# The attention mixer's output product, from float32 matmuls to three products of rounded parts and rests

## The reference, cut to what matters

```python
def attend(qb, k, v):
    s = jnp.einsum('bqhgd,bkhd->bhgqk', qb, k, preferred_element_type=F32) * scale
    p = jax.nn.softmax(s, axis=-1).astype(v.dtype)
    return jnp.einsum('bhgqk,bkhd->bqhgd', p, v)
...
o = lax.map(lambda qb: attend(qb, k_all, v_all), q_blocks)
y_lat = jnp.moveaxis(o, 0, 1).reshape(Bn, L, ATT_HEADS * dh) @ w_out    # 256x1024 times 1024x1024
```

## Time and profile before

| | |
|---|---|
| median of three runs | 2270.58 us |
| the profiled execution | 2269.32 us, of them 2267.5 us span |
| PE busy | 2183.9 us, 96% of the span |
| DVE, ACT busy | 1365.3 us (60%), 957.5 us (42%) |
| DMA | 373.10 MB, 165 GB/s on average |
| granted PE clock over the span | 0.987 |
| attention units, first scores to last mix | 811.2 to 852.5 us |
| output product | 853.3 to 881.2 us |
| feed-forward part begins | 895.3 us |

### The profile page before, as it was taken

One profiled execution on the slowest core, in us unless ns is written; L12 is line 12 of the kernel. 1 busy time (PEld: TensorE's weight loads), 2 busy tenths in 40 slices (PEclk: granted clock), 3 DMA queues, 4 the chain that ended last, 5 costly groups with the idle time before them and its releaser, 6 DMA issues. The chain is left out here.

```text
span 2267.5 us, 32554 instructions
## 1 busy us (share of the span) xinstructions
PE 2183.9 (96%) x13686; PEld 1868.4 (82%) x13686; DVE 1365.3 (60%) x1577; ACT 957.5 (42%) x1078; POOL 124.6 (5%) x69
## 2 busy tenths in 40 slices
PE   6999999999999998999999999999999999989999
PEld 4887788888888767888888898888988897878888
DVE  4357835756856364656665674566656686636665
ACT  3312424445544243444444463444444465234443
POOL 0066500000000000000000000000000011000000
PEclk8999999999999999999999999999999998999999
DMA  8327904554555302555555334554555442124552
GB/s 329 112 93 315 420 28 154 186 185 168 194 191 189 134 25 75 198 190 186 186 185 185 140 130 149 187 185 165 186 185 185 148 168 93 40 84 151 189 191 80
DMA packets 52529, 373.10 MB, mean 165 GB/s; under 512 B 5776, under 2 KB 6800, under 8 KB 7888
## 3 DMA queue, kind: packets, MB, share of 16 engines
q1 hardware_dynamic: 51632, 367.78, 44.7%
q0 software_dynamic: 800, 3.93, 0.5%
HBM read 370.64 MB, written 1.05 MB: 164 GB/s over the span
## 5 line engine op out<-in xcount | busy, mean ns | idle before, releaser
L375 PE MATMUL PS<-AR_r 128*128 128x512 f32 x2240 | 793.1, 398 | 1.5 <-DVE ring_r L502 1.5
L502 DVE TENSOR_TENSOR ring_r<-ring,AR_r 128x2048 fp32r<-128x2048 f32 x270 | 619.2, 2299 | 286.4 <-ACT AR_r L496 286.3
L496 ACT ACTIVATE AR_r<-ring 128x2048 fp32r<-128x2048 f32 x274 | 522.2, 1911 | 311.4 <-PE PS L394 193.6
L376 PE MATMUL PS<-AR_r,ring_r 128*128 128x256 f32 x2240 | 628.2, 280 | 0.0
L375 PEld LDWEIGHTS PS<-AR_r 128*128 128x128 f32 x2240 | 420.8, 188 | 105.4 <-DVE ring_r L502 2.3
L376 PEld LDWEIGHTS PS<-AR_r,ring_r 128*128 128x128 f32 x2240 | 422.8, 189 | 2.4
L554 ACT ACTIVATE AR<-PS 128x512 f32<-128x512 f32 x140 | 83.7, 598 | 439.7 <-PE PS L376 439.7
L392 PE MATMUL PS<-AR_r 128*128 128x512 f32 x616 | 242.3, 393 | 0.0
L394 PE MATMUL PS<-AR_r 128*128 128x512 f32 x616 | 240.9, 391 | 0.0
L393 PE MATMUL PS<-ring_r,AR_r 128*128 128x512 f32 x616 | 240.1, 390 | 0.0
L394 PEld LDWEIGHTS PS<-AR_r 128*128 128x128 f32 x616 | 115.6, 188 | 26.3
(11 more groups left out here) (390 smaller groups left out, 3027.9 us busy)
## 6 DMA issues: line engine op xcount, KB each, us to landing
ring<-stream SPq DMA_DIRECT2D x346, 1024.0 KB, 4.8
X<-xt SPq DMA_DIRECT2D x1, 2048.0 KB, 9.3
AR<-bias POOLq DMA_DIRECT2D x1, 1536.0 KB, 6.6
AR<-pt POOLq DMA_DIRECT2D x2, 512.0 KB, 3.6
out<-X SPq DMA_DIRECT2D x4, 256.0 KB, 2.1
SM<-small SPq DMA_DIRECT2D x1, 545.0 KB, 4.3
AR<-invc SPq DMA_DIRECT2D x1, 512.0 KB, 14.8
X<-negl POOLq DMA_DIRECT2D x1, 512.0 KB, 6.2
```

The source lines that it names most:

```text
L375: pe.matmul(PS[:, bank, :], w_hi, X_PARTS[:, :, k * T:(k + 1) * T], start=(k == 0), stop=False, skip_group_check=True)
L376: ins = pe.matmul(PS[:, bank, 0:T], w_lo, X_HI[:, k, :], start=False, stop=(k == DT - 1), skip_group_check=True)
L496: act.activation(w_hi_of(tag, i), ring[:, n % SLOTS, :], ACT.Identity).then_inc(split_hi, 1)
L502: dve.tensor_tensor(RING_R[:, n % SLOTS, :], ring[:, n % SLOTS, :], w_hi_of(tag, i), ALU.subtract).then_inc(split_lo, 1)
```

## The change

The output product is made from three fp32r products. Its four chunks are laid out anew: chunk 2h + part holds the features 4 part to 4 part + 3 (tiles of 128) by 512 output columns of half h, so that the matmuls are 128 x 512. The mixed heads are rounded by ACT into CAT1_HI (`round_heads`), and DVE writes the rest into CAT1_LO (`take_heads`). All four chunks are split, each with its own place for the rounded part. Chunks 0 and 1 are split in halves between the attention units, chunks 2 and 3 behind them. The two banks of the mixed pairs are exchanged, and PE's order in the product is half of the columns, half of the features, token tile.

```diff
-            if name.startswith(("ffn", "ple")) or name in ("mix0_in", "mix2_in", "mix3_in"):
+            if name.startswith(("ffn", "ple")) or name in ("mix0_in", "mix1_out", "mix2_in", "mix3_in"):
...
+        OUT1_HI = [arena(at, CHUNK_COLS, of=AR_R) for at in (16384, 18432, 20480, 22528)]
...
+        def act_split_half_chunk(act, order, tag, i, half):
+
+            n, cs = START[tag] + i, slice(half * 1024, (half + 1) * 1024)
+            need_chunk(act, n)
+            ins = act.activation(w_hi_of(tag, i)[:, cs], ring[:, n % SLOTS, cs], ACT.Identity)
+            if half:
+                act.wait_ge(order.sem, order.n)
+                ins.then_inc(split_hi, 1)
+            else:
+                ins.then_inc(order.sem, order.step())
...
-        CAT1 = arena(11264, AH, T)
+        CAT1_LO = arena(11264, AH, T, of=AR_R)
+        CAT1_HI = H_R[:, :, LAT]
+        MIX_BANKS = (0, 7)
...
-            pe.wait_ge(S["heads_taken"], S.at("heads_taken", 3))
-            for t in range(2):
-                for h in range(2):
-                    pe_tokens(pe, "mix1_out", "mix1_post", CAT1, 0, t, h, 2 * t + h, t == 1)
+            for h in range(2):
+                for part in range(2):
+                    i = 2 * h + part
+                    pe.wait_ge(split_lo, SPLIT_BASE["mix1_out"] + i + 1)
+                    w_hi, w_lo = OUT1_HI[i], RING_R[:, (START["mix1_out"] + i) % SLOTS, :]
+                    pe.wait_ge(S["heads_taken"], S.at("heads_taken", 2 if i == 0 else 3))
+                    for t in range(2):
+                        ts, o = slice(t * P, (t + 1) * P), PS[:, 2 * t + h, :]
+                        for k in range(4 * part, 4 * part + 4):
+                            w = slice(k % 4 * 512, (k % 4 + 1) * 512)
+                            pe.matmul(o, CAT1_HI[:, k, ts], w_hi[:, w], start=(k == 0), stop=False)
+                            pe.matmul(o, CAT1_HI[:, k, ts], w_lo[:, w], start=False, stop=False)
+                            ins = pe.matmul(o, CAT1_LO[:, k, ts], w_hi[:, w], start=False, stop=(k == DT - 1))
+                        if part and t == 0:
+                            ins.then_inc(S["tokens_done"], S.mark("tokens_done", ("mix1_post", t, h)))
+                    ins.then_inc(multiplied, 1)
...
+                if i in (4, 5, 8, 9):
+                    act_split_half_chunk(act, order, "mix1_out", i // 8, i % 2)
+                if i % 4 == 2 and i > 2:
+                    round_heads(act, i // 4 - 1)
+            round_heads(act, 3)
+            for i in (2, 3):
+                act_split_chunk(act, "mix1_out", i, free=START["mix1_in"])
+
+        def round_heads(act, hp):
+            act.wait_ge(S["head_mixed"], S.at("head_mixed", 2 * hp + 1))
+            act.activation(CAT1_HI[:, 2 * hp:2 * hp + 2, :], PS[:, MIX_BANKS[hp % 2], :].rearrange("p (a b) -> p a b", a=2),
+                           ACT.Identity).then_inc(S["heads_rounded"], S.mark("heads_rounded", hp))
...
+                if i in (5, 6, 9, 10):
+                    dve_split_half_chunk(dve, order, "mix1_out", (i - 5) // 4, (i - 5) % 2)
                 if i % 4 == 2 and i > 2:
                     take_heads(dve, i // 4 - 1)
             take_heads(dve, 3)
+            for i in (2, 3):
+                dve_split_chunk(dve, "mix1_out", i)

         def take_heads(dve, hp):
-            dve.wait_ge(S["head_mixed"], S.at("head_mixed", 2 * hp + 1))
-            dve.tensor_copy(CAT1[:, 2 * hp:2 * hp + 2, :].rearrange("p a b -> p (a b)"), PS[:, (7, 0)[hp % 2], :]).then_inc(S["heads_taken"], S.mark("heads_taken", hp))
+            dve.wait_ge(S["heads_rounded"], S.at("heads_rounded", hp))
+            heads = slice(2 * hp, 2 * hp + 2)
+            dve.tensor_tensor(CAT1_LO[:, heads, :], PS[:, MIX_BANKS[hp % 2], :].rearrange("p (a b) -> p a b", a=2), CAT1_HI[:, heads, :],
+                              ALU.subtract).then_inc(S["heads_taken"], S.mark("heads_taken", hp))
...
+def chunks_out_halves(w):
+
+    return w.reshape(2, 4, P, 2, 512).transpose(3, 0, 2, 1, 4).reshape(4, P, -1)
...
-    parts["mix1_out"] = chunks_in(g["att_w_out"][0])
+    parts["mix1_out"] = chunks_out_halves(g["att_w_out"][0])
```

More of the change, by code:

```diff
@@ L174, in build @@
         TURN_OF = {"ple2b": 2, "ple3b": 2, "ffn4": 1, "mix3_in": 1, "ffn1_lat": 2, "ffn2": 2, "mix2_in": 2}
-        w_hi_of = lambda tag, i: W0_HI[i % 3] if tag == "mix0_in" else W_HI[(i + TURN_OF.get(tag, 0)) % 3]
+        OUT1_HI = [arena(at, CHUNK_COLS, of=AR_R) for at in (16384, 18432, 20480, 22528)]
+        w_hi_of = lambda tag, i: OUT1_HI[i] if tag == "mix1_out" else W0_HI[i % 3] if tag == "mix0_in" else W_HI[(i + TURN_OF.get(tag, 0)) % 3]
         X_HI, X_LO = (arena(at, DT, T, of=AR_R) for at in (12288, 16384))
@@ L1214, in mix @@
                 for st in range(NCH):
-                    ins = pe.matmul(PS[:, (7, 0)[hp % 2], (h % 2) * T:(h % 2 + 1) * T], VV[:, st, (h // 4) * P:(h // 4 + 1) * P],
+                    ins = pe.matmul(PS[:, MIX_BANKS[hp % 2], (h % 2) * T:(h % 2 + 1) * T], VV[:, st, (h // 4) * P:(h // 4 + 1) * P],
                                     PT[:, h % 2, st, :], start=(st == 0), stop=(st == NCH - 1))
```

## The result

The kernel after takes 2275.51 us in the median of 7 runs (2272.05 to 2278.48), against 2270.58 before; the two medians lie 4.9 apart. The ratio on record is 1.0030, with a 95% interval of 1.0021 to 1.0039: 6.8 us slower, with 4.8 and 8.9 as the ends. Its profiled execution took 2277.11 us with a span of 2275.3; that of before 2269.32 and 2267.5.

The account below looks back on a forecast made before the run. PE alone bounds the output product, a PE-DVE loop the units. Units +8.4, product and earlier start -6.7, two clock falls +5.0: +6.7 us, 2277 us; own range 2274.5 to 2280, over the cases 8 in 10 between 2270 and 2281.

Parts of the forecast that it names:

- the falls: Clock drops to half speed after the long waits at units 5 and 9: two, 2.5 us each, 5.0 together; chance 0.60.
- The bound: Attention units: a loop through PE, DVE's maxima and scaling, 4.80 us for two units; work put between those lengthens it fully.
- The product: Output product: 96 matmuls at 0.230 us, as in the feed-forward row of the same form, take 5.7 us less.
- the start: Output product begins 1.04 us earlier, at 852.26 instead of 853.30, since its first quarter needs only the third pair of heads.
- The units: Attention units: added splits and pairs' rests delay PE by 3.19 + 0.52 + 3.16 + 0.52 + 1.0 = 8.4 us.
- The sum without falls: Delay in the units less the product's gain, clock drops left out: 8.4 - 6.7 = +1.7 us.
- The 3.6 us of idle time: PE idle at unit 5 from the end of unit 8's scores to 830.97; held long enough to bring a clock drop.
- the other five: Idle stretches of 2.8 to 4.7 us in PE's work in the trace; clock drops followed three of the five.
- half speed from 830.97 for 6.8 us: Price of a clock drop from unit 6's transposes on: 2.5 us each, bounds 1.5 and 3.4.
- 13.4: Sign in the timeline: the last mix that many us later than 850.53 with the clock drops, 8.4 without.
- the tail from 881.24 on stays as it is: Behind the product's last sums: remaining rounding, rests and chunks are done before them, so nothing was added there.
- the idle-time one: Rival: DVE's halves fit its 1.96 us waits before the maxima; only unit 14 costs 1.0, 5.7 us faster, 2264.9; chance 0.05.

Follow-up runs that it names:

- e4: The changed kernel with ACT's list alone altered: its halves of the first two chunks come after units 2, 4, 5 and 8; 2269.83 us, ratio 1.0005.
- e3: The changed kernel reordered: only the first chunk split between units, DVE's halves and two pairs' rests ahead of the maxima; 2267.36 us, ratio 0.9989.
- e1: The changed kernel with three filler score matmuls on PE in each long wait, before the transposes of units 6 and 10; 2273.48 us, ratio 1.0018.
- e8: The order of e3 with two filler score matmuls on PE between the last mix and the product; 2267.24 us, ratio 0.9996.
- e7: The kernel before, run again unaltered for a second timeline; one run, 2272.77 us.
- e9: The kernel before with two filler score matmuls on PE ahead of its product; 2270.31 us, ratio 1.0004.
- e2: The changed kernel without half chunks between the units: chunk 0 split ahead of the last pair, 1 to 3 behind it; 2269.04 us, ratio 1.0003.
- e5: e3 run once more, unchanged; 2266.40 us in 11 runs, ratio 0.9986.
- e6: e3 with six filler score matmuls on PE: two ahead of the transposes behind the product, four behind the norm's sums; 2260.86 us, ratio 0.9959.

## Why the prediction was right, point by point

The time came out where it was forecast, 2275.5 for 2277.0, and the ratio's 6.8 us are the forecast's 6.7. That the middle was hit so closely is in part luck: the falls were priced at more than twice what they cost, and some 3 us that lie outside of the stretch (6.8 less 3.5; 1.4 by the medians), which the forecast put at nothing, fill the gap.

- **The bound.** The loop through maxima and scaling was the right reading: DVE and ACT have idle time, and all that is put between maxima and scaling shows on PE in full. e4 shows it: DVE's 1.15 us of work costs 1.14. e3 is the test from the other side: with one chunk's halves and two pairs' rests ahead of the maxima (after has two chunks' halves in the loop) the units cost nothing.
- **The product.** 5.75 less for 5.7, the start 1.13 earlier for 1.04, from a row of the same form. The Trainium skill ("TensorE: Matmul & The Clock Gate", "Back-to-back issue gap") gives about 131 ns for a matmul of 512 columns in a stream with weight loads. The trace doesn't agree, with 96 in 22.2 us, 0.23 each.
- **The units.** Unit 6 is turned 3.03 late for 3.19, of it by e4 1.89 of waiting for ACT and 1.14 of DVE's work; the step behind it takes another 0.51 for 0.52 (e1's 5.32 less 4.81); units 10 and 11 alike; unit 15 0.98 for 1.0. Together 8.06 for 8.4. The sum without falls is then 8.06 - 6.88 = 1.18, and e1's stretch shows just that.
- **The falls.** That both long waits would bring one was right, and in e1, with PE at work in the waits, none came. The 3.6 us of idle time that the forecast held against the other five are 3.46 in the measure in which these are given; 3.30 came, and the comparison stands. The Trainium skill ("TensorE: Matmul & The Clock Gate", "HAM oscillation — how this bites in real kernels") says that a burst behind idle time starts cold. The trace agrees only in part: here the clock fell 1.4 and 0.8 us into the bursts, not at their start. The mis-sized term is "half speed from 830.97 for 6.8 us", 2.5 per fall: it measured 3.4 us and 1.17, below the lower bound of 1.5. Half of 3.4 is 1.7, and part of it is hidden: the 0.69 for which PE waits before the transposes of unit 7 in e1 are gone in after. No fall in the trace of before lasts less than 6.8 (the one at the span's end is cut off by it), so the length couldn't have been read there. Two falls cost 2.35, not 5.0, so the stretch is 3.5 longer, not 6.7, and the last mix comes 10.4 later behind the first scores, not 13.4. With this size the forecast's own sum gives +4, 2274.6, the bottom of its range.
- **The rest.** The forecast held that "the tail from 881.24 on stays as it is" and so put nothing for it. By its order it does stay: 2.84 us of waiting as before. But the clock fell there too, which cost 2.1 in this execution; it did so in e1, e4 and e8 as well (0.8, 2.0 and 0.8), and not in before, e7, e9, e2, e3 and e5, behind the same wait. So neither the wait nor the rounded product decides it, and the cause is open. 1.4 more lie behind the feed-forward's start and 0.8 ahead of the mixer, where the instructions are those of before. The 0.8 lie within what two executions of before differ by (3.4 at that place); the 1.4 don't, since before, e7 and e9 agree there within 0.23. Their cause is open too, as is that of e1's 3 us beyond its stretch.

Of the rivals, the idle-time one is refuted at the point that it named: the half's wait for ACT wasn't over when the negative maxima were done. But with another order its idea is right, as the stretch of e3 shows.

## What to carry to other kernels

In a loop through several engines' lists, idle time of an engine is usable only on the side on which the engine waits: put extra work ahead of the instruction that waits (here the maxima), not between it and what the next engine wants. When an estimate includes a fall of the clock, a fall elsewhere in the trace doesn't give its price: here one lasted half as long and was partly hidden. Measure it with and without filler matmuls. Judge a change of some microseconds by the stretch between two fixed instructions as well as by the total: here a stretch repeated within 0.01 us while a lead of 6.8 arrived at the end as 2.5. And when a forecast's total comes out, check its terms all the same.

## What the runs showed of the hardware that was not expected

- The same 2.84 us of idle time was followed by full clock in before and by half clock in after and in e4.
- Falls lasted 3.4 us here and 6.8 at the feed-forward of before, and one came with PE at work, 2.1 us behind an idle time of only 0.92 (e5 at 1978).
- PE stopped for 0.92 us in a row of matmuls with nothing in the profile that it waited for (e3, e5), where before ran through the same row.
- The same program's first scores came at 811.21 and at 814.61 us in two executions: the later one has a fall of 6.8 at 228 that the other lacks. Low clock far ahead of a change moved the total by nearly as much as the change to the stretch.
- Six filler matmuls made a kernel 5.5 us faster (e6 against e5), 3.5 more than the full clock that they bring to the feed-forward beside them was expected to be worth.
